# Sixteen weight-sum transfers moved between the scalings of an attention stage, and the transposed input stored in its natural layout

## The reference

```python
h = rmsnorm(x, norm1_g)                     # x: 1024 prompt rows and 8 sample rows, 1024 wide
z = h @ w_in                                # the input of all three mixers
p_s = masked_softmax(q @ k.T)               # full (causal) branch, gated per head
p_w = masked_softmax(q @ k_win.T)           # sliding window of 512, gated per head
o_n = g0 * o_c + g1 * (p_s @ v) + g2 * (p_w @ v)
x = x + concat(o_g, o_n, o_m) @ w_out       # needs the input x again
hid = relu(rmsnorm(x, norm2_g) @ w_up)
x = x + (hid * hid) @ w_down                # w_down: 4096 x 1024
```

## Time and profile before

| | |
|---|---|
| median of 3 runs | 1828.91 us (1822.0 to 1833.11) |
| the profiled execution | 1834.37 us, of which the span is 1832.7 us |
| PE busy | 1671.5 us, 91% of the span |
| DVE, ACT, POOL busy | 1135.6, 734.4, 288.4 us |
| mean granted clock of PE | 0.948 of full speed |

### The profile page before, as it was taken

The page is one execution under the profiler, slowest core; times in us unless marked ns, Lnnn a source line. Parts: engine busy times, 40 slices in busy tenths (PEclk is TensorE's granted clock), DMA queues, the critical chain, the costliest instruction groups (busy, mean ns, idle before and its releaser), DMA issues. The chain is left out here.

```text
span 1832.7 us, 34713 instructions
## 1 busy us (share of the span) xinstructions
PE 1671.5 (91%) x13909; PEld 1539.2 (84%) x13909; DVE 1135.6 (62%) x1886; ACT 734.4 (40%) x1379; POOL 288.4 (16%) x380
## 2 busy tenths in 40 slices
PE   6799999980999997999997699799999989999997
PEld 6699999970888885788873499699999989999997
DVE  6264386230887775666677669877777775555531
ACT  6343342120665554444445234333333344443431
POOL 1000000021222223422221232121211120000000
PEclk7899999985999998999998799899999999999999
DMA  7851155359915233677588463254454488665641
GB/s 169 113 122 36 34 152 163 128 196 341 206 29 93 51 89 111 216 238 239 179 227 205 159 197 99 68 175 135 146 167 134 139 290 280 195 198 177 192 138 53
DMA packets 290910, 287.47 MB, mean 157 GB/s; under 512 B 61166, under 2 KB 243014, under 8 KB 288126
## 3 DMA queue, kind: packets, MB, share of 16 engines
q1 hardware_dynamic: 263278, 179.79, 34.8%
q0 software_dynamic: 25088, 100.94, 17.8%
q10 hardware_dynamic: 2384, 4.53, 1.1%
HBM read 215.36 MB, written 107.60 MB: 176 GB/s over the span
## 5 line engine op out<-in xcount | busy, mean ns | idle before, releaser
L59 PE MATMUL pm<-ops,slots 128*128 128x258 f32 x1792 | 510.0, 285 | 19.8 <-DVE ops L3664 14.8
L60 PE MATMUL pm<-ops,slots 128*128 128x258 f32 x1792 | 508.4, 284 | 0.0
L61 PE MATMUL pm<-ops,slots 128*128 128x258 f32 x1792 | 507.4, 283 | 0.0
L59 PEld LDWEIGHTS pm<-ops,slots 128*128 128x128 f32 x1792 | 339.5, 189 | 20.9 <-DVE ops L3664 15.5
L61 PEld LDWEIGHTS pm<-ops,slots 128*128 128x128 f32 x1792 | 341.9, 191 | 0.0
L60 PEld LDWEIGHTS pm<-ops,slots 128*128 128x128 f32 x1792 | 341.7, 191 | 0.0
L59 PE MATMUL pz<-hH,winH 128*128 128x344 f32 x600 | 201.0, 335 | 1.6 <-DVE hL L850 1.6
L60 PE MATMUL pz<-hL,winH 128*128 128x344 f32 x600 | 194.7, 324 | 0.0
L61 PE MATMUL pz<-hH,winL 128*128 128x344 f32 x600 | 194.6, 324 | 0.0
L3670 DVE TENSOR_TENSOR slots<-uact,slots 128x512 fp32r<-128x512 f32 x160 | 109.7, 699 | 77.8 <-ACT slots L3490 77.7
L3490 ACT ACTIVATE slots<-uact 128x512 fp32r<-128x512 f32 x160 | 99.0, 625 | 126.9 <-DMA uact<-in_w_down_dram 40.0
(11 more groups left out here) (682 smaller groups left out, 3386.7 us busy)
## 6 DMA issues: line engine op xcount, KB each, us to landing
hidD_scratch<-onat POOLq DMA_DIRECT2D x112, 258.0 KB, 3.3
downS_scratch<-in_w_down_dram POOLq DMA_DIRECT2D x12, 2048.0 KB, 50.7
hs<-hidD_scratch SPq DMA_DIRECT2D x38, 516.0 KB, 5.0
uact<-in_w_up_dram SPq DMA_DIRECT2D x64, 256.0 KB
uact<-downS_scratch SPq DMA_DIRECT2D x64, 256.0 KB, 3.0
raw<-in_w_in_dram SPq DMA_DIRECT2D x24, 512.0 KB, 3.8
uact<-in_w_down_dram SPq DMA_DIRECT2D x48, 256.0 KB, 3.9
wo<-hidD_scratch SPq DMA_DIRECT2D x18, 516.0 KB, 4.5
```

The source lines that it names most:

```text
L59: nc.tensor.matmul(out, wH, mH, start=start and k == 0, stop=False)
L60: nc.tensor.matmul(out, wH, mL, start=False, stop=False)
L61: last = nc.tensor.matmul(out, wL, mH, start=False, stop=stop and k == n - 1)
```

## The change

In the attention stage the twelve half-transfers that stood ahead of the first scaling, and the four later ones, are spread: one half ahead of each of the 7th and 8th sliding step (copy of sum 0), 11th and 12th (copy of sum 2), 16th and 17th (add to sum 0), 21st and 22nd (copy of sum 1), 26th and 27th (copy of sum 3), 31st and 32nd (add to sum 2), 37th and 38th (add to sum 1), 43rd and 44th (add to sum 3). The adds keep their waits. In the projection stage a tile of `xT` is stored at column 128 t, and the samples in one DMA of eight columns. In the mixer each half is loaded by four DMAs: two of 256 columns and two of 2 columns.

```diff
 def store_x(t):
+    n = P if t < TQ else NS
     sp.wait_ge(xt_copied, 2 * t + 2)
-    if t < TQ:
-        at = (t // 2) * (TT // 4) + (t % 2) * P
-        sp.dma_start(xTd[:, :, at:at + P], xTr[t % 7][:, :, :]).then_inc(xt_stored[min(t, 2)], 16)
-    else:
-        for q in range(4):
-            at = (q + 1) * (TT // 4) - 2
-            sp.dma_start(xTd[:, :, at:at + 2], xTr[t % 7][:, :, 2 * q:2 * q + 2]).then_inc(xt_stored[min(t, 2)], 16)
+    sp.dma_start(xTd[:, :, t * P:t * P + n], xTr[t % 7][:, :, 0:n]).then_inc(xt_stored[min(t, 2)], 16)
...
-copy_sum(0, down_quarter(1, 0))
-copy_sum(2, down_quarter(0, 0))
-copy_sum(1, down_quarter(0, 0))
-copy_sum(3, down_quarter(0, 1))
-add_sum(0, down_quarter(1, 1))
-add_sum(1, down_quarter(1, 0))
 sliding = [s for s in range(len(sched.steps)) if sched.steps[s][1] == WIN]
 for s in range(len(sched.steps)):
-    if s == sliding[len(sliding) // 2]:
-        pool.wait_ge(sums_done[0], 64)
-        add_sum(2, io["downS"][0])
...
+    for n in range(2):
+        if s == sliding[6 + n]:
+            copy_sum(0, down_quarter(1, 0), n)
+        if s == sliding[10 + n]:
+            copy_sum(2, down_quarter(0, 0), n)
+        if s == sliding[15 + n]:
+            add_sum(0, down_quarter(1, 1), n)
...
+        if s == sliding[42 + n]:
+            pool.wait_ge(sums_done[2], 64)
+            add_sum(3, io["downS"][2], n)
...
-sp.dma_start(x2[0], xT[:, :, 0:2 * CQ]).then_inc(x_in[0], 16)
+def load_x(c):
+    for h in range(2):
+        q = 2 * c + h
+        sp.dma_start(x2[c][:, :, h * CQ:h * CQ + 2 * P], xT[:, :, 2 * q * P:2 * (q + 1) * P]).then_inc(x_in[c], 16)
+        sp.dma_start(x2[c][:, :, h * CQ + 2 * P:(h + 1) * CQ], xT[:, :, T + 2 * q:T + 2 * q + 2]).then_inc(x_in[c], 16)
+load_x(0)
...
-dve.wait_ge(x_in[c], 16)
+dve.wait_ge(x_in[c], 64)
```

More of the change, by code:

```diff
@@ L256, in _ @@
                 sp.wait_ge(xt_stored[1], 16)
-                sp.wait_ge(xt_stored[2], 16 * (TQ + 2))
+                sp.wait_ge(xt_stored[2], 16 * (TQ - 1))
                 sp.dma_start(gi, zT[MI:MI + 4, 0:T]).then_inc(rows_in, 16)
@@ L1307, in down_quarter, with copy_sum, add_sum @@
                     return w_down[j * 2 * D:(j + 1) * 2 * D, i * 512:(i + 1) * 512]
[L1309 to L1314, removed]
+                def copy_sum(f, block, n):
+                    rows = slice(n * D, (n + 1) * D)
+                    nc.gpsimd.dma_start(io["downS"][f, rows, :], block[rows, :], max_dma_last_dim=2048).then_inc(sums_done[f], 16)
+                def add_sum(f, block, n):
+                    rows = slice(n * D, (n + 1) * D)
                     pool.wait_ge(sums_done[f], 32)
-                    for n in range(2):
-                        rows = slice(n * D, (n + 1) * D)
-                        nc.gpsimd.dma_start(io["downS"][f, rows, :], block[rows, :], accum_op=ALU.add, max_dma_last_dim=2048).then_inc(sums_done[f], 16)
+                    nc.gpsimd.dma_start(io["downS"][f, rows, :], block[rows, :], accum_op=ALU.add, max_dma_last_dim=2048).then_inc(sums_done[f], 16)
                 def scale_sliding(s):
@@ L1338, in _ @@
                 ahead_at = [s for s in range(len(sched.steps)) if sched.steps[s][1] == WIN and sched.units[sched.steps[s][0]][0] == BLOCK_ORDER[-1]][3]
-                copy_sum(0, down_quarter(1, 0))
-                copy_sum(2, down_quarter(0, 0))
-                copy_sum(1, down_quarter(0, 0))
-                copy_sum(3, down_quarter(0, 1))
-                add_sum(0, down_quarter(1, 1))
-                add_sum(1, down_quarter(1, 0))
                 sliding = [s for s in range(len(sched.steps)) if sched.steps[s][1] == WIN]
                 for s in range(len(sched.steps)):
-                    if s == sliding[len(sliding) // 2]:
-                        pool.wait_ge(sums_done[0], 64)
-                        add_sum(2, io["downS"][0])
-                    if s == sliding[3 * len(sliding) // 4]:
-                        pool.wait_ge(sums_done[2], 64)
-                        add_sum(3, io["downS"][2])
+                    for n in range(2):
[5 more added lines that the diff above has]
+                            add_sum(0, down_quarter(1, 1), n)
+                        if s == sliding[20 + n]:
+                            copy_sum(1, down_quarter(0, 0), n)
+                        if s == sliding[25 + n]:
+                            copy_sum(3, down_quarter(0, 1), n)
+                        if s == sliding[30 + n]:
+                            pool.wait_ge(sums_done[0], 64)
+                            add_sum(2, io["downS"][0], n)
+                        if s == sliding[36 + n]:
+                            add_sum(1, down_quarter(1, 0), n)
+                        if s == sliding[42 + n]:
+                            pool.wait_ge(sums_done[2], 64)
+                            add_sum(3, io["downS"][2], n)
                     if s == ahead_at:
@@ L3202, in _ @@
                         sp.wait_ge(nsaL_ready, TQ + 1)
-                        sp.dma_start(x2[1], xT[:, :, 2 * CQ:4 * CQ]).then_inc(x_in[1], 16)
+                        load_x(1)
                     if v == 7:
```

## The result

The changed kernel takes 1776.38 us (median of 4 runs, 1771.73 to 1782.01), beside 1829.34 for the kernel before (4 runs): a ratio of 0.9717 (95% interval 0.9675 to 0.9758), 2.8% faster, about 52 us. The forecast was 1774. Its profiled execution took 1776.86 us, of which the span is 1774.8, at a mean granted clock of 0.966 (before 0.948).

What follows compares the result with a forecast made beforehand. PE, busy 91% of the span, was taken as the bound, with long waits in attention and projection. Terms -43 - 13.3 + 1.5 = -54.8 took 1834.4 to 1779.6; that execution being 5.5 above the median, forecast 1774 us, range 1762 to 1790.

Steps and rivals of the forecast that it cites:

- The stall: Attention: PE's 46.9 us wait for POOL's first scaling shrinks to 1.8, 45.1 saved; net -43, from -45 to -39.
- the lost lead: Attention's first short blocks: DVE no longer gets ahead of PE during the stall; charged 2 us, ends 0 and 6.
- the gain I had left out: Attention: the shorter gap may spare some of PE's nine microseconds at half clock; not counted.
- The sums' new places: Attention: sixteen spread issues, 0.8 us a copy and 1.3 an add, delay nobody: 0, or 16 us without cover.
- The stores: Projection: aligned tile stores all go at 292 GB/s; PE's 11.3 us wait and 2.0 of slow clock go: -13.3.
- The step that was said not to be proved by one trace: Projection stores: the byte offset of later tiles causes the lower rate, 143 against 292 GB/s.
- Rival 1: Projection: store pace doesn't depend on offset; only three saved issues count, 2 us gap stays, -9.5, 1778 us; chance 0.23.
- The loads in the mixer: Mixer: split loads with 8-byte pieces, 1.2 us each, delay weight columns by 0.4 to 4.2; +1.5, ends 0 and 7.
- The sum: Whole kernel: -43 - 13.3 + 1.5 = -54.8 against the profiled 1834.4 us; forecast 1774 us.
- The sums' part: Attention: net -43 for the stall, with 0 for the spread sums at their new places.
- The input's part: Projection and mixer: -13.3 for the stores and +1.5 for the mixer loads.

Runs made afterwards that it cites:

- kernel 1: Only the sum transfers spread, the transposed input's storing and loading as in the kernel before: 1784.09 us, ratio 0.976 against the kernel before.
- kernel 5: Changed kernel with rows of `xT` 4160 bytes apart, content at offset 0 (also called `rows padded, offset 0`): 1775.88 us, ratio 0.9735 against the kernel before.
- kernel 6: Changed kernel with rows of `xT` 4160 bytes apart and content moved by 8 bytes: 1782.61 us, ratio 0.9772 against the kernel before.
- kernels 3 and 4: Each against the changed kernel: 3 issues all eight copies ahead of the first scaling, 1775.31 us; 4 loads each mixer half by one DMA, 1770.04 us.
- kernel 7: Changed kernel with rows of `xT` 4160 bytes apart and content moved by 32 bytes: 1776.8 us in one run.
- 10: Changed kernel with the second half's x loads issued behind the weight columns of step 9: 1772.47 us, ratio 0.971 against the kernel before.
- input only: Only the transposed input's storing and loading changed, sums ahead of the first scaling as in the kernel before: 1820.26 us, ratio 0.9971 against it.

## Why the prediction was right, step by step

**The stall: right in mechanism and size.** The remaining wait for POOL is 1.7 us, forecast 1.8. The net of -43 stands against -43.8 (ratio) or -41.5 (medians) in time (kernel 1) and -44.2 in the stage, a mean of 279.5 over the ten kernels with spread sums, against 323.7 for the two that have the stall (326.6 and 320.8). The profile before and after alone would give -48.9; nearly 3 of that is the clock ahead of the wait, told above. Whether 2 us was the right charge for the lost lead can't be read within this scatter. The half-clock stretch got shorter, 6 us instead of nine, the gain I had left out, and a few tenths of PE idle stand in its place between 400 and 405 us.

**The sums' new places: right.** 0.8 to 1.0 us for a copy and 1.3 to 1.4 for an add, forecast 0.8 and 1.3, and no wait of POOL on `downS`. The rule of the Trainium skill that I weighed (SBUF — State Buffer, section "SBUF: two separate sides") would have added 2.5 us to each moved issue, an estimate from that page's two figures. Here the four issues of POOL shown above, made while DVE worked (9.46 of the 10 us from 410 on), took 0.82 to 1.38 us, so the trace doesn't show that cost in this kernel; whether DVE's instructions there were of the kind that the rule speaks of, no run here shows.

**The stores: right, and now proved.** The step that was said not to be proved by one trace was the offset. Kernels 5 and 6 differ in it alone and in nothing else, and the pace falls by more than 40%. The time line came out as worked: SP through the stores at 47.8 us (forecast 49), the small load issued at 56.9 (57.3), PE busy at full clock from 60 to 72 us. Forecast for the stage -13.3; measured -12.1: attention starts at 376.9 on average over the ten kernels with whole, aligned stores, at 389.0 over the two with the stores of before. Rival 1 falls: with nine issues but the low pace a wait of 7.2 us was left, not 2. With twelve issues it was 11.3 (before) and 8.9 (kernel 1), so the three saved issues alone bring 2 to 4 us and the offset the other 7. What the forecast had too large is the worth of this part in time, see the sum. The page of the Trainium skill that stood on its side (DMA: Bandwidth & Descriptors, section "How a descriptor splits into AXI transactions") would have 17 beats in place of 16 for a piece that starts off a 256-byte boundary. With rows 4128 or 4160 bytes apart most pieces do that at any of these offsets, so by the page kernels 5 and 6 would hardly differ. The measured pace over 38 to 48 us, 165 against 288 GB/s, is far from that, and the measurement decides.

**The loads in the mixer: the place wrong, the size near.** Forecast +1.5, from weight columns that come 0.4 to 4.2 us late for the products of step 9. An 8-byte DMA kept SP for 0.7 and 2.8 us (and 1.1 and 3.9 in the first half) where I took 1.2; the columns were asked for about 5 us later behind the same neighbours, and ACT waited 7.5 us instead of 5.9. Yet PE didn't stop at the products. It stopped 1.7 us for POOL's sum of squares, through a chain that the prediction didn't name: ACT's queue holds the square of step 7 behind the split of step 9's columns. By the stage's means the price is 1.8 us (146.1 over the eight kernels with four loads at step 8, 144.3 over the three with one load a half), by the medians of kernels 3 and 4 it is 5. Whether it is 2 or 5 stays open; that moving the loads away took the wait but no measurable time speaks for the small one.

**The sum: near, with some luck.** -54.8 was forecast against the profiled execution; the two profiled executions differ by 57.5, and the medians of the runs by 53 (52 by the ratio). The sums' part came out as forecast. The input's part, forecast at -11.8 with its price in the mixer, brought 5.3 us alone (2.0 to 8.8 by its interval) and about 8 on top of the sums, where the stages say 12.1 less about 2. What accounts for the rest stays open. The one trace of before may mislead here: its execution took 1834.37 us, nearly 9 more than the median of the 13 runs beside kernels 1 to 4, so the stages read from it can be too long.

## What to carry to other kernels

When an engine's queue holds both short work that others wait for and transfers that wait for earlier transfers, it is the waits to land that cost, not the issues: leave the copies where they are if need be, and put each add as far behind its copy as the copy takes to land (12.8 us here behind the second half's issue, about four steps). Look at the byte offset of every piece stored to DRAM: a transfer split into more and odder pieces elsewhere may be the lesser price. And behind a load that comes late, look at everything queued behind the instruction that waits for it, since another engine may be held by that and not by the load.

## What the runs showed of the hardware

Stores of 512-byte pieces to DRAM, from 38 to 48 us: 284 to 291 GB/s where all pieces began at a multiple of 64 bytes from the start of the scratch (kernel 5), 267 where all began 32 bytes behind one (kernel 7), 138 to 203 with an offset of 8 bytes (kernel 6), all at a DMA share of about 1.2. In the changed kernel, whose rows are 4128 bytes apart, half the rows are of the first kind and half of the second, and the 275 to 279 of its two traces lie midway. The DMA share therefore doesn't tell a fast stream from a slow one here; GB/s does. Why 8 bytes cost so much no run shows.

SP's issue of a transfer took 0.3 to 0.6 us where little was queued ahead of it (0.37 for the whole of the second half's x in before), and up to 3.9 us for a load of 8-byte pieces behind another such load (first half's x in after).

The clock that PE is granted in the first 30 us isn't the same from run to run. Windows 10 to 20 us, of before and of after:

```profile
10.00:20.00 10.00, 5.44 (x27) 4.89 (x28) 8.33 (x9) 9.97 (x18) 0.00 (x0) 0.62 0.58 198
```

```profile
10.00:20.00 10.00, 4.98 (x26) 4.43 (x27) 8.21 (x9) 9.97 (x18) 0.00 (x0) 0.77 0.59 206
```

Nothing of the change reaches this stretch. In five of the other kernels' traces the clock is 1.00 there (kernels 4, 5, 6, 7 and 10). It doesn't set when attention starts: `input only` has 0.66 in this window and starts at 375.0, `rows padded, offset 0` has 1.00 and starts at 375.6.
